# Moving the rows of the normalised x, both halves, to 64 bytes under a multiple of 1024 bytes

## The chip, the core and the metric

The kernel runs on one core of a Trainium2 chip. The metric is the time of one execution on the device in microseconds (us), lower is better; the figure of a kernel is the median of its runs.

## The reference

Two transformer blocks of two layers each, run one after the other on x (512 tokens of width 1024, fp32). The second block also carries a context of 256 tokens. Each sublayer normalises its input, scales and shifts it by vectors made from c, and multiplies the result by wide weight matrices. Cut to what the change touches:

```
h = rms_norm(x, g_norm1[l]) * (1.0 + sc1) + sh1          # block 1, attention part
u = h @ w_in[l] + b_in[l]
...
h = rms_norm(x, g_norm2[l]) * (1.0 + sc2) + sh2          # block 1, feed-forward part
up = causal_depthwise_conv(h @ w_up[l], w_conv[l], b_conv[l])
...
hx = rmsnorm(x, norm_g[i, 0]) * (1.0 + sc_x) + sh_x      # block 2, on x and on the context
hc = rmsnorm(ctx, norm_g[i, 0]) * (1.0 + sc_c) + sh_c
yx = conv_module(hx, *cp)                                # layer 0; attention in layer 1
...
fx = rmsnorm(x, norm_g[i, 2]) * (1.0 + scf_x) + shf_x
x = x + gf_x * rmsnorm(swiglu(fx, ffn_w1[i], ffn_w3[i], ffn_w2[i]), norm_g[i, 3])
```

## The kernel before, in words

Activations lie with their channels on the 128 partitions: x is `X`, eight rows (KD = 8 blocks of 128 channels) of 512 tokens in each partition. A row here is one such block in one partition, 512 fp32 numbers, 2048 bytes. The normalised x is kept as two fp32r tiles, a rounded half `Hh` and the rest `Hl` (lines 185 and 187), so that a product of fp32 accuracy is made of three fp32r matmuls:

```
def three(o, wh, wl, xh, xl, start, stop):                                      # line 433
    pe.matmul(o, wh, xh, start=start, stop=False, skip_group_check=True)        # line 435
    pe.matmul(o, wh, xl, start=False, stop=False, skip_group_check=True)        # line 436
    return pe.matmul(o, wl, xh, start=False, stop=stop, skip_group_check=True)  # line 437
```

Here a weight block of 128 columns (`wh` or `wl`, 512 bytes of a partition) is loaded into TensorE and a row of `Hh` or `Hl` moves through it; the output is one PSUM bank. A slab of weights (128 output channels, eight such blocks) comes by a DMA that SP issues into one of three `raw` tiles; ACT rounds it into `Wh` (line 2045), GpSimd (line 2534) or VectorE (line 1274) makes the rest, `Wl`. `linear` (line 449) runs the 8 x 3 matmuls of one slab on x. `linear_pair` (line 497) does two slabs at once behind a normalisation.

In the second block the context has its own halves, `hc_h` and `hc_l`, 256 tokens, rows of 1024 bytes (line 221). `linear_both` (line 466) takes, for each weight block, three matmuls on x (512 columns) and then three on the context (256 columns); `linear_pair_both` (line 477, called four times) takes x first and then the context. The feed-forward product of the second block's layer 0 has x and context side by side in one row of 768 numbers, `gb_h` and `gb_l` (line 272), and takes 512 and 256 columns of it in turn. The last attention turns its weights p into `pt2_hi` and `pt2_lo` (lines 287 and 288; pt_hi and pt_lo in the profile), rows of 256 numbers, which lie over `Hh` when that is free; the products with v are lines 1135 and 1136. GpSimd scales p (line 2579).

The places of the tiles are set by hand in one block of lines. `alloc_sbuf_tensor` puts one tile behind the other; `at` and `alloc_sbuf_tensor_at` put tiles of other stages at fixed places over them.

```
ROW = SEQ * 2                                              # line 182: 1024
assert nc.sbuf_base % ROW == 0, nc.sbuf_base               # line 183
X = sb("X", [KD, SEQ])                                     # line 184
Hh = sb("Hh", [KD, SEQ], F32R)
hl_base = nc.sbuf_base
Hl = sb("Hl", [KD, SEQ], F32R)
...
LINE = 64 / KB                                             # line 220
HC = {c0: [at(f"hc_{x}{c0}", kb - LINE, [KD, CTX], F32R) for x, kb in (("h", c0), ("l", c0 + 8))] for c0 in (0, 56)}
```

In the built program X begins at byte 27648 of each partition, Hh at 44032, Hl at 60416 and raw0 at 76800, all multiples of 1024. Wh and Wl, gb, pt_hi and pt_lo begin on multiples of 1024 too. The four hc tiles begin 64 bytes under one. The tiles `hl_base` places besides: four of the eight first weight tiles w0 (line 223), two of the five p buffers (line 281), pt_hi and pt_lo, and the tiles XT and YT of the output (lines 291 and 292).

Of the kernel before, what the change touches and what calls it, by code (L numbers as in the profile page):

```python
# [31 lines left out]
class Tally:  # L32
# [17 lines left out]
    def mark(self, name, *event, by=1):  # L50
        self.raised[name] = self.raised.get(name, 0) + by
        assert (name, event) not in self.at, (name, event)
        self.at[name, event] = self.raised[name]
        return self.sems[name], by

    def ready(self, name, *event):
        if self.known is None:
            return self.sems[name], self.at.get((name, event), 1)
        return self.sems[name], self.known[name, event]
# [34 lines left out]
def write(nc, a, out, tally):  # L94

    mark, ready = tally.mark, tally.ready
    _, SEQ, D = a["x"].shape
    CTX = a["ctx_2"].shape[1]
    DEPTH = a["w_in"].shape[0]
    KD = D // P  # L100
# [13 lines left out]
    C_QL, C_KV, C_KR, C_Q, C_K, C_V, C_GM, C_GS, _ = CUTS  # L114
# [6 lines left out]
    def sb(name, shape, dt=F32):  # L121
        return nc.alloc_sbuf_tensor(name, [P, *shape], dt)
# [3 lines left out]
    cvec = {1: sb("cvec1", [1, KD]), 2: sb("cvec2", [2, KD])}  # L126
    cact = {1: sb("cact1", [KD, 1]), 2: sb("cact2", [KD, 2])}
    MOD = {(b, l): sb(f"mod{b}_{l}", [6 * KD, b]) for b in (1, 2) for l in range(DEPTH)}
    DER = {(b, l): sb(f"der{b}_{l}", [4 * KD, b]) for b in (1, 2) for l in range(DEPTH)}


    vec_at, vec_rows = {}, []
# [36 lines left out]
    def vec(name, i=0, n=1):  # L169
        c = vec_at[name] + i  # L170
        return vcols[:, c:c + n]
# [8 lines left out]
    tap_cols = sb("tap_cols", [4, QUADS, KD])  # L180

    ROW = SEQ * 2
    assert nc.sbuf_base % ROW == 0, nc.sbuf_base
    X = sb("X", [KD, SEQ])
    Hh = sb("Hh", [KD, SEQ], F32R)
    hl_base = nc.sbuf_base
    Hl = sb("Hl", [KD, SEQ], F32R)
    RAW, WS, TM = 3, 3, 3
    raw = [sb(f"raw{i}", [8 * P]) for i in range(RAW)]
    Wh = [sb(f"Wh{i}", [8 * P], F32R) for i in range(WS)]  # L190
# [18 lines left out]
    def at(name, kb, shape, dt=F32):  # L209
        size = int(np.prod(shape)) * 4  # L210
        assert kb * KB + size <= 80 * KB, name
        return nc.alloc_sbuf_tensor_at(name, [P, *shape], dt, offset=int(base + kb * KB))
# [4 lines left out]
    XC = at("XC", 72, [KD, CTX])  # L217
    XS = {"x": X, "c": XC}
    STATS = {"x": (SV, SY, ST, SR), "c": tuple(at(f"ctx_stat{i}", 51 + i, [CTX]) for i in range(4))}
# [109 lines left out]
    def full(job):  # L329
        return ready("bank_full%d" % bank_of[job], *job)  # L330

    def free(job):
        return tally.sems["bank_free%d" % bank_of[job]], use_of[job]
# [4 lines left out]
    def empty(job):  # L338
        return tally.sems["bank_free%d" % bank_of[job]], 1

    def bank(job, n=SEQ):
        if n > SEQ:
            return banks2(job, n)
        return PS[:, bank_of[job], 0:n]

    def banks2(job, n):
        b = bank_of[job]
        return PS[:, b:b + 2, :].rearrange("p b n -> p (b n)")[:, 0:n]
# [49 lines left out]
    def _(pe):  # L398
# [287 lines left out]
        def to_tokens(job, src):  # L686

            begin(job)
            for t in range(QT):
                mm = pe.transpose(bank(job)[:, t * P:(t + 1) * P], src[:, t * P:(t + 1) * P], const("ident"))  # L690
            mm.then_inc(*fill(job))

        def last_turns(j):
# [5 lines left out]
            else:  # L699
                i = len(tally.squares) % 2  # L700
                tally.squares.append(ev)
                tally.square_free[ev] = lambda: ready("sums", ev) if j < KD - 1 else full(job)
            to_tokens(("xt", j), X[:, j, :])
            if j > 0:
# [541 lines left out]
    def _(dve):  # L1246
# [14 lines left out]
        def own(inst):  # L1261
            chain_n[0] += 1
            return after(inst, "dve_chain", chain_n[0])
# [12 lines left out]
        def mod_work(slab_n):  # L1276

            while mod_events and mod_events[0][2] <= slab_n:
                what, block_of, _, r = mod_events.pop(0)
                if what == "sum":  # L1280
                    mod_sum(block_of, r)
                else:
                    (mod_row_out if what == "row" else mod_columns)(block_of)
# [123 lines left out]
        def mod_out(b, l):  # L1407

            while any(e[1][0:2] == (b, l) for e in mod_events):
                mod_work(mod_events[0][2])  # L1410
            M, R = MOD[b, l], DER[b, l]
            dve.wait_ge(*free(("mod_t", b, l, MOD_BLOCKS - 1)))
# [9 lines left out]
        def gain(o, m, g, plus):  # L1422
            if plus:
                return own(dve.scalar_tensor_tensor(o, m, 1.0, g, ALU.add, ALU.mult))
            return own(dve.tensor_tensor(o, m, g, ALU.mult))
# [30 lines left out]
        def col(b, l, s, what, c):  # L1456
            v = 1 if s == "c" else 0
            if what < 6:
                return MOD[b, l][:, what * KD + c, v:v + 1]
            return DER[b, l][:, (what - 6) * KD + c, v:v + 1]  # L1460

# [283 lines left out]
        def mask(name):  # L1745
            return const(name).bitcast(F32)
# [33 lines left out]
        def first_gains():  # L1780
# [3 lines left out]
            dve.wait_ge(*free(("mod_t", 1, 0, 0)))  # L1784
            dve.wait_ge(*gain(DER[1, 0][:, 0:KD, 0], MOD[1, 0][:, KD:2 * KD, 0], vec(("g1", 0), 0, KD), True))

        for l in range(DEPTH):
# [83 lines left out]
            for n in range(len(tiles) + 4):  # L1871
                if n < len(tiles):
# [5 lines left out]
                    dve.wait_ge(*own(dve.tensor_tensor(d, d, mask("mask_qk"), ALU.add)))  # L1878
                    t = own(dve.tensor_reduce(mx[n % 3], bank(("s", l, h, i), (i + 1) * P), AX.X, ALU.max))
                    dve.wait_ge(*t)  # L1880
# [43 lines left out]
            def add_to_x(job, g, j):  # L1924
                dve.wait_ge(*full(job))
                dve.scalar_tensor_tensor(X[:, j, :], bank(job), g, X[:, j, :], ALU.mult, ALU.add).then_inc(*empty(job))

# [56 lines left out]
        for n in range(len(tiles) + 10):  # L1984
            if n < len(tiles):
                job = ("s2", *tiles[n])
                dve.wait_ge(*full(job))
                if n >= 3:
                    dve.wait_ge(*free(("s2", *tiles[n - 3])))
                dve.tensor_reduce(nm[n % 3], banks2(job, SEQ + CTX), AX.X, ALU.min).then_inc(*mark("neg_max2", *tiles[n]))  # L1990
            if 11 <= n < len(tiles) + 8 and n % QT == 3:
# [34 lines left out]
    def _(act):  # L2026
# [40 lines left out]
        def square(event, src, n, rows=slice(0, P), bias=0.0):  # L2067
            if event[1] == KD - 2 and ("ss", event[0]) in sums_over:
                ln_and_exp()
            if event[0] in SUMMED and event[1] == 0:  # L2070
                job = ("ss", event[0])
                if sums_over[job][1]:
                    act.wait_ge(*sums_over[job][1])
                act.activation(STATS[stream(job)][0][:, 0:n], src, ACT.Square, bias=bias).then_inc(*mark("squares", event))
                return
            i = sq_n[0]
            assert tally.squares[i] == event, (tally.squares[i], event)
            if i >= 2:
                act.wait_ge(*tally.square_free[tally.squares[i - 2]]())
            act.activation(SQ[i % 2][rows, 0:n], src, ACT.Square, bias=bias).then_inc(*mark("squares", event))  # L2080
            sq_n[0] += 1
# [117 lines left out]
        def ffn_2(l, s):  # L2199
            n, tag, name = NS[s], ("f", l, s), ("dn", 2, l, s)  # L2200
            norm_to_h(tag, n, lambda c: col(2, l, s, 3, c))
            for half in range(2):
# [11 lines left out]
                for j in range(KD):  # L2214
# [5 lines left out]
                    else:  # L2220
# [3 lines left out]
                        if j >= 2:  # L2224
                            act.wait_ge(*full(("yt", j - 2)))
                        act.activation(sl[j % 2][:, :], Y[:, j, :], ACT.Identity, scale=DER[2, l][:, 3 * KD + j, 0:1])\
                           .then_inc(*mark("y_gained", j))
# [77 lines left out]
        for l in range(DEPTH):  # L2305
# [132 lines left out]
            for j in range(KD):  # L2438
# [3 lines left out]
                act.wait_ge(*free(("wo", l, j)))  # L2442
                square((("n2", l), j), X[:, j, :], SEQ)

# [253 lines left out]
```

## Time and profile before

| what | value |
|---|---|
| median of 3 runs | 3287.12 us (3286.65 to 3288.83) |
| span of the profiled execution | 3282.0 us; its own total is not listed apart |
| TensorE busy | 3152.4 us, 96% |
| VectorE, ScalarE, GpSimd busy | 1570.4, 1186.3, 815.1 us |
| matmuls on Hh or Hl | 3 x 2208, of 512 columns |
| matmuls on hc_h or hc_l | 3 x 576, of 256 columns |

The span runs from the first to the last instruction; the time of a run also has what lies around it. The busy time of matmuls is a union: they overlap, and the duration of one (about 390 ns for 512 columns) is longer than the distance between the starts of two. The distance is read in the timeline, whose columns are the start in us from the span's begin, the duration in us, the engine, the line, the operation, output <- inputs (the moving operand first, then the weights) and the shape.

### The profile page before, as it was taken

Reading aid. Unit: us, or ns where it says so; the run is one execution under the profiler, and the core shown is the slowest. Engines: PE = TensorE matmul, PEld = TensorE weight load, DVE = VectorE, ACT = ScalarE, POOL = GpSimd, SP = SyncE. Lnnn points to the kernel's source line nnn. Section 1 sums busy time; section 2 is a strip of 40 time slices with the busy share of each in tenths; the row PEclk is TensorE's granted clock in tenths of the full one; section 3 lists DMA queues with packets and bytes.
Section 4 is the critical chain, followed back from the end, with each engine's and each line's share of the span. In section 5 each row is a group of like instructions: output and inputs, shape, how many; then the busy total and the mean of one; then the engine's idle time right before and its main releaser. Section 6 shows DMA issues by size and latency. Waiting matters only on the chain.

```text
span 3282.0 us, 38620 instructions
## 1 busy us (share of the span) xinstructions
PE 3152.4 (96%) x15546; PEld 2472.2 (75%) x15546; DVE 1570.4 (48%) x2204; ACT 1186.3 (36%) x1764; POOL 815.1 (25%) x399
## 2 busy tenths in 40 slices
PE   6999999999999999999989899999999979999998
PEld 4657778887665777778867477888888658878887
DVE  3572146464375124334378644322334899653234
ACT  3443244243444224424321244111112558632223
POOL 4302445555320343444401000000000039500000
PEclk9999999999999999999999999999999999999999
DMA  6413436665430555453335211222221110122332
GB/s 237 129 42 110 147 91 200 217 192 164 128 113 7 180 175 171 144 178 93 98 81 130 53 49 55 65 65 65 61 62 58 39 39 1 39 70 88 106 89 79
DMA packets 429892, 337.21 MB, mean 103 GB/s; under 512 B 16637, under 2 KB 411223, under 8 KB 417428
## 3 DMA queue, kind: packets, MB, share of 16 engines
q1 hardware_dynamic: 428272, 334.23, 33.5%
q8 instruction: 124, 2.03, 0.3%
q0 software_dynamic: 1248, 0.46, 0.1%
q14 instruction: 52, 0.43, 0.0%
q10 hardware_dynamic: 196, 0.07, 0.0%
HBM read 319.58 MB, written 2.10 MB: 98 GB/s over the span
## 4 chain that ended last, share of the span: by engine, by line
PE 58%; DVE 5%; POOL 4%; ACT 1%; issue 1%; SPq 0%; DMA 0%; POOLq 0%; DVEq 0%; ACTq 0%
PE PS L435 17%; PE PS L436 17%; PE PS L437 17%; POOL p L2579 4%; PE PS L524 1%; PE PS L831 1%; PE PS L592 1%; PE PS L637 1%; DVE both_tmp L1371 0%; DVE q_parts L1693 0%; PE PS L1026 0%; DVE Wl L1274 0%; PE PS L536 0%; DVE stat_t L1347 0%; SPq L2621 0%
## 5 line engine op out<-in xcount | busy, mean ns | idle before, releaser
L435 PE MATMUL PS<-Hh,Wh 128*128 128x512 f32 x2208 | 875.4, 396 | 20.5 <-DVE both_tmp L1371 8.3
L2534 POOL TENSOR_TENSOR Wl<-raw,Wh 128x1024 fp32r<-128x1024 f32 (+2 forms) x254 | 618.0, 2441 | 986.6 <-ACT Wh L2045 986.6
L436 PE MATMUL PS<-Hl,Wh 128*128 128x512 f32 x2208 | 861.8, 390 | 0.0
L437 PE MATMUL PS<-Hh,Wl 128*128 128x512 f32 x2208 | 861.4, 390 | 0.0
L2045 ACT ACTIVATE Wh<-raw 128x1024 fp32r<-128x1024 f32 (+2 forms) x442 | 436.1, 988 | 400.4 <-PE PS L437 349.5
L435 PEld LDWEIGHTS PS<-Hh,Wh 128*128 128x128 f32 x2208 | 416.1, 188 | 127.9 <-issue 62.6
L437 PEld LDWEIGHTS PS<-Hh,Wl 128*128 128x128 f32 x2208 | 415.8, 188 | 88.0
L436 PEld LDWEIGHTS PS<-Hl,Wh 128*128 128x128 f32 x2208 | 416.4, 189 | 67.6 <-issue 3.4
L1274 DVE TENSOR_TENSOR Wl<-raw,Wh 128x1024 fp32r<-128x1024 f32 (+3 forms) x188 | 217.6, 1157 | 389.6 <-ACT Wh L2045 389.3
L1952 DVE SCALAR_TENSOR_TENSOR cv<-PS,vcols,cv 128x510 f32<-128x510 f32 (+1 forms) x176 | 123.7, 744 | 216.8 <-ACT cv L2456 216.8
L435 PE MATMUL PS<-g_h,Wh 128*128 128x512 f32 x528 | 206.7, 391 | 3.5 <-POOL Wl L2534 3.5
L2564 POOL CAST k_hi<-k_ctx 64x512 fp32r<-64x512 f32 x4 | 3.6, 911 | 813.2 <-DVE k_ctx L1371 813.1
L437 PE MATMUL PS<-g_h,Wl 128*128 128x512 f32 x528 | 205.6, 389 | 0.0
L436 PE MATMUL PS<-g_l,Wh 128*128 128x512 f32 x528 | 205.5, 389 | 0.0
L435 PE MATMUL PS<-hc_h,Wh 128*128 128x256 f32 x576 | 162.7, 282 | 0.9 <-DVE hc_l L1429 0.8
L436 PE MATMUL PS<-hc_l,Wh 128*128 128x256 f32 x576 | 161.8, 281 | 0.0
L437 PE MATMUL PS<-hc_h,Wl 128*128 128x256 f32 x576 | 161.8, 281 | 0.0
L2579 POOL TENSOR_SCALAR p<-p,small 128x768 f32<-128x768 f32 x64 | 141.8, 2234 | 49.6 <-DVE small L2002 49.6
L524 PE MATMUL PS<-sq,cst 128*128 128x512 f32 (+2 forms) x244 | 119.9, 611 | 33.2 <-DVE stat_v L1344 17.6
L2456 ACT ACTIVATE cv<-PS,vcols 128x512 f32<-128x512 f32 x88 | 68.5, 779 | 192.5 <-PE PS L437 189.2
L435 PEld LDWEIGHTS PS<-hc_h,Wh 128*128 128x128 f32 x576 | 108.1, 188 | 22.5 <-DVE hc_l L1429 1.9
L436 PEld LDWEIGHTS PS<-hc_l,Wh 128*128 128x128 f32 x576 | 108.2, 188 | 20.2
(383 smaller groups left out, 4759.3 us busy)
## 6 DMA issues: line engine op xcount, KB each, us to landing
raw<-in_ffn_w SPq DMA_DIRECT2D x108, 512.0 KB, 3.6
mod_w<-in_w_mod SPq DMA_DIRECT2D x48, 1024.0 KB, 5.0
raw<-in_w_up SPq DMA_DIRECT2D x88, 512.0 KB, 4.6
mod_w<-in_w_ada SPq DMA_DIRECT2D x40, 1024.0 KB, 4.9
raw<-in_w_in SPq DMA_DIRECT2D x62, 512.0 KB, 4.0
UQ<-U SPq DMA_DIRECT2D x128, 99.4 KB, 2.2
raw<-in_w_down SPq DMA_DIRECT2D x32, 384.0 KB, 5.0
raw<-in_conv_w_pw SPq DMA_DIRECT2D x24, 512.0 KB, 4.1
```

The lines of the kernel that those rows point to most:

```text
L435: pe.matmul(o, wh, xh, start=start, stop=False, skip_group_check=True)
L436: pe.matmul(o, wh, xl, start=False, stop=False, skip_group_check=True)
L437: return pe.matmul(o, wl, xh, start=False, stop=stop, skip_group_check=True)
L524: mm = pe.matmul(bank(job, n), const(matrix)[lo:hi, :], SQ[i][lo:hi, 0:n], start=first, stop=final, skip_group_check=True)
L592: pe.matmul(PS[:, b, :], const("ident"), cst[:, 0:512], start=True, stop=True)
L637: mm = pe.matmul(PS[32 * j:32 * j + b, bank_of[job], :], cact[b][:, r, :], w[:, 512 * j:512 * (j + 1)], start=r == 0, stop=r == KD - 1, sk ...
L1274: dve.tensor_tensor(low, src, high.bitcast(F32), ALU.subtract).then_inc(*mark("w_low", k))
L1952: ins = dve.scalar_tensor_tensor(o, bank(ups[s])[:, 0:SEQ - lag], vec(("w_conv", l), tap * 2 * FC + s * FC + f), o, ALU.mult, ALU.add)
L2045: act.activation(high, src, ACT.Copy).then_inc(*mark("w_high", k))
L2456: act.activation(cv[f % 2][s][:, :], bank(job), ACT.Identity, bias=vec(("b_conv", l), s * FC + f), scale=vec(("w_conv", l), 2 * 2 * FC + s ...
L2534: pool.tensor_tensor(low, src, high.bitcast(F32), ALU.subtract).then_inc(*mark("w_low_pool", one[0]))
L2579: pool.tensor_scalar(p2[n % 5][:, :], p2[n % 5][:, :], ri2[n % 5], None, ALU.mult)\
```

## The change

Hh and Hl begin 64 bytes (16 fp32 numbers) under a multiple of 1024. The room for it comes from `der1_0` and `der1_1`, which had twice the columns they use. X, which follows the small tiles directly, begins 128 bytes lower than before; a filler of 64 bytes stands between X and Hh, another of 64 bytes behind Hl, and from raw0 on every tile is where it was.

```
--- before.py
+++ after.py
@@ -126,7 +126,7 @@
     cvec = {1: sb("cvec1", [1, KD]), 2: sb("cvec2", [2, KD])}
     cact = {1: sb("cact1", [KD, 1]), 2: sb("cact2", [KD, 2])}
     MOD = {(b, l): sb(f"mod{b}_{l}", [6 * KD, b]) for b in (1, 2) for l in range(DEPTH)}
-    DER = {(b, l): sb(f"der{b}_{l}", [4 * KD, b]) for b in (1, 2) for l in range(DEPTH)}
+    DER = {(b, l): sb(f"der{b}_{l}", [2 * b * KD, b]) for b in (1, 2) for l in range(DEPTH)}
 
 
     vec_at, vec_rows = {}, []
@@ -180,11 +180,14 @@
     tap_cols = sb("tap_cols", [4, QUADS, KD])
 
     ROW = SEQ * 2
-    assert nc.sbuf_base % ROW == 0, nc.sbuf_base
     X = sb("X", [KD, SEQ])
+    BELOW = 16
+    sb("rows_begin_below", [-nc.sbuf_base % ROW // 4 - BELOW])
     Hh = sb("Hh", [KD, SEQ], F32R)
     hl_base = nc.sbuf_base
     Hl = sb("Hl", [KD, SEQ], F32R)
+    sb("weights_begin_at", [BELOW])
+    assert nc.sbuf_base % ROW == 0, nc.sbuf_base
     RAW, WS, TM = 3, 3, 3
     raw = [sb(f"raw{i}", [8 * P]) for i in range(RAW)]
     Wh = [sb(f"Wh{i}", [8 * P], F32R) for i in range(WS)]
```

In the built program X begins at byte 27520, Hh at 43968, Hl at 60352, raw0 at 76800. Of the tiles ahead of X, der1_1, der2_0, der2_1, vcols, small and tap_cols begin 64 to 128 bytes lower. Tiles placed by `hl_base` move by 64 bytes with Hl. The instructions, their order on each engine and their waits are the same.

## Rows read from the trace of the kernel before

**Rows 1.** Page, parts 1 and 2: engines busy, granted clock in 40 slices.
```profile
PE 3152.4 (96%) x15546; PEld 2472.2 (75%) x15546; DVE 1570.4 (48%) x2204; ACT 1186.3 (36%) x1764; POOL 815.1 (25%) x399
...
PEclk9999999999999999999999999999999999999999
```

**Rows 2.** Page, part 5: the three groups of matmuls on Hh and Hl.
```profile
L435 PE MATMUL PS<-Hh,Wh 128*128 128x512 f32 x2208 | 875.4, 396 | 20.5 <-DVE both_tmp L1371 8.3
...
L436 PE MATMUL PS<-Hl,Wh 128*128 128x512 f32 x2208 | 861.8, 390 | 0.0
L437 PE MATMUL PS<-Hh,Wl 128*128 128x512 f32 x2208 | 861.4, 390 | 0.0
```

**Rows 3.** Timeline of TensorE, 2910 to 2940 us (start, us, ...); 134 rows.
```profile
2909.77 0.39 PE L436 MATMUL PS<-Hl,Wh 128*128 128x512 f32 x1
...
2939.91 0.39 PE L437 MATMUL PS<-Hh,Wl 128*128 128x512 f32 x1
```

**Rows 4.** Windows: span and us, busy us of PE, PEld, DVE, ACT, POOL, PEclk, DMA.
```profile
2910.00:2940.00 30.00, 30.00 (x134) 24.85 (x133) 13.94 (x15) 11.39 (x14) 0.00 (x0) 1.00 0.36 105
```

**Rows 5.** Timeline of all engines from 2920 us: matmuls and weight loads.
```profile
2920.19 0.39 PE L437 MATMUL PS<-Hh,Wl 128*128 128x512 f32 x1
2920.20 0.19 PEld L435 LDWEIGHTS PS<-Hh,Wh 128*128 128x128 f32 x1
...
2920.42 0.39 PE L435 MATMUL PS<-Hh,Wh 128*128 128x512 f32 x1
2920.42 0.19 PEld L436 LDWEIGHTS PS<-Hl,Wh 128*128 128x128 f32 x1
```

**Rows 6.** Timeline of TensorE, 1672 to 1676.3 us; 39 rows.
```profile
1671.76 0.28 PE L437 MATMUL PS<-hc_h,Wl 128*128 128x256 f32 x1
...
1676.23 0.28 PE L436 MATMUL PS<-hc_l,Wh 128*128 128x256 f32 x1
```

**Rows 7.** Timeline of TensorE, 2762.6 to 2765.3 us; eight rows between these.
```profile
2763.80 0.28 PE L1136 MATMUL PS<-pt_lo,v_parts 128*128 128x256 f32 x1
...
2764.88 0.60 PE L1115 MATMUL PS<-cst,p 128*128 128x128 f32 x4
```

**Rows 8.** Page, part 5: making the weight halves; matmuls on g_h.
```profile
L2534 POOL TENSOR_TENSOR Wl<-raw,Wh 128x1024 fp32r<-128x1024 f32 (+2 forms) x254 | 618.0, 2441 | 986.6 <-ACT Wh L2045 986.6
...
L2045 ACT ACTIVATE Wh<-raw 128x1024 fp32r<-128x1024 f32 (+2 forms) x442 | 436.1, 988 | 400.4 <-PE PS L437 349.5
...
L435 PE MATMUL PS<-g_h,Wh 128*128 128x512 f32 x528 | 206.7, 391 | 3.5 <-POOL Wl L2534 3.5
```

**Rows 9.** Chain that ended last, in order of time: its longest piece.
```profile
2692.89 135.27 POOL p L2579 x61
```

**Rows 10.** Instructions of line 2579: duration min/median/max in ns.
```profile
L2579 POOL TENSOR_SCALAR p<-p,small x64: 2194/2202/2573, 2690.3 to 2830.3; 128x768 f32<-128x768 f32 x64
```

**Rows 11.** Groups of VectorE, shapes apart: making Hl.
```profile
L1387 DVE SCALAR_TENSOR_TENSOR Hl<-tmp,mod,Hh 128x512 fp32r<-128x512 f32 x48 | 35.9, 747 | 2.8 <-ACT Hh L2115 1.9
...
L1387 DVE SCALAR_TENSOR_TENSOR Hl<-both_tmp,mod,Hh 128x512 fp32r<-128x512 f32 x16 | 12.0, 747 | 8.5 <-ACT Hh L2115 8.2
```

**Rows 12.** Timeline of TensorE, 2016 to 2030 us: gb, six matmuls a step.
```profile
2018.16 0.28 PE L435 MATMUL PS<-gb_h,Wh 128*128 128x256 f32 x1
...
2018.51 0.40 PE L435 MATMUL PS<-gb_h,Wh 128*128 128x512 f32 x1
...
2029.00 0.40 PE L435 MATMUL PS<-gb_h,Wh 128*128 128x512 f32 x1
```

**Rows 13.** Timeline of TensorE, 1676.6 to 1690 us: Hh, Hl and hc alternating.
```profile
1676.47 0.39 PE L435 MATMUL PS<-Hh,Wh 128*128 128x512 f32 x1
...
1677.15 0.28 PE L435 MATMUL PS<-hc_h,Wh 128*128 128x256 f32 x1
...
1677.50 0.39 PE L435 MATMUL PS<-Hh,Wh 128*128 128x512 f32 x1
...
1689.90 0.39 PE L435 MATMUL PS<-Hh,Wh 128*128 128x512 f32 x1
```

More of the change, by code:

```diff
@@ L128, in write @@
     MOD = {(b, l): sb(f"mod{b}_{l}", [6 * KD, b]) for b in (1, 2) for l in range(DEPTH)}
-    DER = {(b, l): sb(f"der{b}_{l}", [4 * KD, b]) for b in (1, 2) for l in range(DEPTH)}
+    DER = {(b, l): sb(f"der{b}_{l}", [2 * b * KD, b]) for b in (1, 2) for l in range(DEPTH)}
     vec_at, vec_rows = {}, []
@@ L182, in write @@
     ROW = SEQ * 2
-    assert nc.sbuf_base % ROW == 0, nc.sbuf_base
     X = sb("X", [KD, SEQ])
+    BELOW = 16
+    sb("rows_begin_below", [-nc.sbuf_base % ROW // 4 - BELOW])
     Hh = sb("Hh", [KD, SEQ], F32R)
@@ L187, in write @@
     Hl = sb("Hl", [KD, SEQ], F32R)
+    sb("weights_begin_at", [BELOW])
+    assert nc.sbuf_base % ROW == 0, nc.sbuf_base
     RAW, WS, TM = 3, 3, 3
```

## The prediction

> **What bounds the kernel now.** Read the page's first part and its slices first [rows 1]: TensorE is busy for 3152.4 of 3282.0 us, and its clock is granted at 9 tenths or more in all 40 slices, the upper of its two levels, 2.4 GHz. No other engine is busy for half the span. So the question is not who waits, but what one matmul costs. The costliest groups say which ones [rows 2]: the three lines of `three` with Hh or Hl as the moving operand, 2208 each, 6624 matmuls of 512 columns in all. Their mean of 390 to 396 ns is latency, not pace; matmuls overlap. The pace is the distance between two starts, and for that one reads the timeline. In an undisturbed stretch [rows 3] 134 such matmuls start between 2909.77 and 2939.91 us: 30.14 us / 133 = **226.6 ns each**. TensorE is busy for 30.00 of the 30 us from 2910 on [rows 4]: it waits for nothing there.
>
> Beside each of them the next 128 columns of weights are loaded: the load for the following matmul starts within 0.01 us of the running one [rows 5]. So there are always two streams out of SBUF, the moving row and a weight block, both of which begin on multiples of 512 bytes in the kernel before.
>
> **What a row's place is worth, by the rows there are.** No 512-column fp32r matmul of this kernel starts 64 bytes under a multiple of 1024, so the new price has to come from neighbours.
> - 256 columns from rows 64 bytes under (hc): 39 starts from 1671.76 to 1676.23 us [rows 6], 4.47 / 38 = 117.6 ns.
> - 256 columns from rows on a multiple of 1024 (pt_hi, pt_lo): nine steps from 2763.80 to 2764.88 us [rows 7], 120.0 ns.
>
> Between 226.6 ns for 512 and 120.0 ns for 256 aligned columns lie 106.6 ns for 256 columns, 2.4 columns per ns, which is the granted clock. What is left is a fixed 13.4 ns per aligned matmul at either width. The rows 64 bytes under have 117.6 - 106.6 = 11.0 ns. The difference, 2.4 ns per matmul, is the only price of this edit that the trace offers.
>
> **The change part by part.**
> 1. *Hh and Hl move by 64 bytes.* The moving rows of 6624 matmuls change their place. I take the 2.4 ns of the 256-column rows for the 512-column ones, since the fixed part was the same 13.4 ns at both widths: 6624 x 2.4 ns = **15.9 us less**. All of it lies on the path: in the stretch of [rows 3, 4] TensorE has no gap to lose it in, and what feeds it has room. A slab of weights carries 24 matmuls, 24 x 226.6 ns = 5.44 us before and 5.38 us after; its two halves take ACT 0.99 us and GpSimd 2.44 us [rows 8]. The only group of this kind that shows idle time for a weight half is another product's (g_h), 3.5 us in all [rows 8]; the matmuls on Hh waited 20.5 us, for Hh and Hl themselves [rows 2]. The bounds: nothing gained, if the 2.4 ns belong to something else than the rows' place; at most about one and a half times as much (24 us), if the wider rows gain more. On the other side the loss is bounded by the dearest rows of 512 columns, below.
> 2. *pt_hi and pt_lo lie over Hh and move too*: 384 matmuls of 256 columns, at 2.4 ns 0.9 us. I count nothing. They stand in the last attention, where the chain goes through GpSimd's scaling of p for 135.27 us [rows 9]; TensorE could be quicker there for nothing. Two of that operation's five p buffers move as well (26 of 64 calls). Its calls last 2194 to 2573 ns round a median of 2202 [rows 10]. If every moved call were as slow as the slowest, 26 x 0.37 us = 9.6 us would be lost; VectorE shows no such effect, so I take 0.
> 3. *X moves by 128 bytes, der, vcols, small and tap_cols by up to 128, two of the initial weight tiles and the output rows by 64.* For VectorE the trace has both kinds: making Hl out of tmp, whose tiles begin on multiples of 1024, takes 747 ns, and out of both_tmp, two of whose three tiles begin 64 and 128 bytes past one, 747 ns too [rows 11]. So 0 for every elementwise operation on X, Hh and Hl; most of them run beside matmuls anyway.
> 4. *der1 loses unused columns, two fillers come in.* No instruction comes, goes or changes its queue or its wait; every engine issues what it issued, in the same order.
>
> The sum: 3282.0 - 15.9 = 3266.1 us of span. The median of the three runs, 3287.12 us, lies 5.1 us above the span of the profiled execution, whose own total is not listed. With the same 5.1 us on top the forecast is **3271 us**.
>
> **The rival of no effect.** The 2.4 ns may not be the place's. The aligned 256-column rows come from bursts of twelve, with the same weights twice in a row, and there is a second aligned sample that says otherwise: the 256-column halves of gb are aligned, and three of them take 2018.16 to 2018.51 us, 0.35 us [rows 12]. Three of hc, 64 bytes under, take 1677.15 to 1677.50, also 0.35 [rows 13]. If the fixed part of a 512-column matmul has nothing to do with where its row begins, the time stays at **3287 us**. Against it: the pace in gb is uneven and an aligned burst settles at 120.0 ns.
>
> For this rival speaks a rule. The Trainium skill, "TensorE: Matmul & The Clock Gate", Part 2 (step 1, LDWEIGHTS), says that TensorE reads the moving operand and the weights through two independent SBUF ports, so that a weight load takes nothing from a running matmul. By that rule two streams never meet, no offset between them matters, and the sum would be 3287. The same page gives a warm back-to-back gap of columns / 2.4 + 2.5 ns, about 216 ns for 512; the trace has 226.6 ns, so something beyond its formula is paid for here on every matmul.
>
> **The rival that ends slower.** The rows of hc may be cheap not because they lie 64 bytes under a boundary, but because they lie off the rows of Hh between which they are taken. `linear_both` alternates three matmuls of 512 columns on x with three of 256 on the context. Thirteen such sixes take 1676.47 to 1689.90 us [rows 13], 1033 ns each. In gb, where both kinds begin on multiples of 1024, ten sixes take 2018.51 to 2029.00 us [rows 12], 1049 ns each. Since three narrow ones take 0.35 us in both, those 16 ns sit on the 512-column ones. After the change Hh and hc have the same place again. If equality is what hurts, each of the 512 interleaved sixes (576 groups of three on hc, less 4 x 16 that `linear_pair_both` runs by themselves) pays 16 ns: 8.2 us more, **3295 us**, while plain stretches keep 226.6 ns. It decides if the pace in a six goes above 1042 ns. A harsher form is that 512-column rows off the boundary lose those 16 ns per three everywhere: 2208 x 16 ns = 35 us, **3322 us**. For both: the dear 512-column rows exist, and no trace shows a 512-column row off the boundary that is cheap. Against both: in a stretch of hc alone, where all rows have the same place, the pace is 117.6 ns and not dearer.
>
> That the change doesn't do what it says can be left out: the built program has Hh at byte 43968 and Hl at 60352 of each partition, 64 under 43 and 59 times 1024, and the weights where they were.
>
> **How the numbers follow.** A measurement of this kernel can tell some 0.2% from no change, 6.6 us: faster is under 3280.5 us, slower over 3293.7. The forecast of a cheaper fixed part has 0.45, since the two cleanest stretches of equal width differ in just this; its own range is 3263 (one and a half times the price) to 3279 (half of it), with some 0.05 for a larger gain. No effect has 0.25, for the equal 0.35 us in the two mixed stretches. The sixes that pay again have 0.18, the loss in all 512-column rows 0.12. So faster 0.45, same 0.25, slower 0.30. The range goes from 3259 to 3300: it takes in the first three cases with a few us on either side for parts 2 and 3, and leaves out the loss everywhere and a gain well above the price, 0.17 together.
>
> **What would show it.** In the timeline of a stretch like [rows 3], the distance of starts on Hh and Hl: 224.2 ns if the forecast holds, 226.6 if there is no effect, 230 or more in the harsh case. In sixes of Hh and hc: 1026 ns by the forecast, 1033 without effect, 1049 by the slower rival. In gb nothing moves, so its 1049 ns has to stay; that is the check that a difference comes from the rows' place. The scaling of p should keep its median of 2202 ns. The forecast is wrong if the pace of 512 columns stays or rises, or if it falls and the span does not follow, which would mean that TensorE was not what bound those stretches.

## The result and the profile after

The changed kernel takes 3319.34 us (median of four runs, 3317.29 to 3320.74) against 3287.97 us of the kernel before on the same chip: a ratio of 1.0095, 95% interval 1.0081 to 1.0109. It is slower by 31.4 us, by the interval 26.6 to 35.8 us. The forecast was 3271 us, the range ended at 3300: wrong in sign. The harsher form of the second rival had 3322 us.

The profiled execution has a span of 3315.5 us and took 3317.29 us itself. Three lines were added ahead of the helpers, so line 435 is now 438, and so on. The page's parts 1, 2 and 4, beside [rows 1], and behind them part 4 of the kernel before (shares of the span in the chain of work that ended last):

```profile
PE 3191.5 (96%) x15546; PEld 2477.4 (75%) x15546; DVE 1571.8 (47%) x2204; ACT 1188.0 (36%) x1764; POOL 807.6 (24%) x399
...
PEclk9999999999999999999999999999999989999999
...
PE 61%; DVE 6%; ACT 2%; issue 1%; SPq 0%; POOL 0%; DMA 0%; DVEq 0%; ACTq 0%
```

```profile
PE 58%; DVE 5%; POOL 4%; ACT 1%; issue 1%; SPq 0%; DMA 0%; POOLq 0%; DVEq 0%; ACTq 0%
```

TensorE is busy 39.1 us longer; GpSimd is busy 7.5 us less, the rest within 5.2 us of before. The chain went through GpSimd's scaling of p for 4% of the span before; now GpSimd has 0% of it, and TensorE 61% for 58%. One slice of the clock has an 8, and the mean granted clock is 0.985, where it was 0.987. The profile of the first experiment below has such a slice too and 0.984, and it is not slower, so the clock is not the cause. The time is in the matmuls. Their groups, beside [rows 2] and the one on g_h in [rows 8] (g_h did not move):

```profile
L438 PE MATMUL PS<-Hh,Wh 128*128 128x512 f32 x2208 | 885.9, 401 | 18.0 <-DVE both_tmp L1374 8.3
L440 PE MATMUL PS<-Hh,Wl 128*128 128x512 f32 x2208 | 875.1, 396 | 0.0
L439 PE MATMUL PS<-Hl,Wh 128*128 128x512 f32 x2208 | 875.0, 396 | 0.0
...
L438 PE MATMUL PS<-g_h,Wh 128*128 128x512 f32 x528 | 206.7, 392 | 3.4 <-POOL Wl L2537 3.4
```

The three groups on Hh and Hl are longer by 5 to 6 ns a matmul, the one on g_h by 1 ns. No wait has grown: the idle time ahead of L438 is 18.0 us, where it was 20.5. The pace, in the timeline of the same stage as [rows 3] (134 rows again), and the windows of that stretch, to be read beside [rows 4]:

```profile
2942.99 0.39 PE L438 MATMUL PS<-Hh,Wh 128*128 128x512 f32 x1
...
2974.03 0.39 PE L439 MATMUL PS<-Hl,Wh 128*128 128x512 f32 x1
```

```profile
2943.00:2973.00 30.00, 30.00 (x130) 24.07 (x129) 11.60 (x13) 9.39 (x12) 0.00 (x0) 1.00 0.36 106
```

31.04 us / 133 = **233.4 ns**, where it was 226.6. TensorE is again busy for all of the 30 us at full clock, and 130 matmuls fit where 134 did. The other stretches of the prediction, in the timeline of the kernel after:

```profile
1695.32 0.28 PE L440 MATMUL PS<-hc_h,Wl 128*128 128x256 f32 x1
...
1700.08 0.28 PE L440 MATMUL PS<-hc_h,Wl 128*128 128x256 f32 x1
...
1701.24 0.39 PE L438 MATMUL PS<-Hh,Wh 128*128 128x512 f32 x1
...
1714.80 0.39 PE L438 MATMUL PS<-Hh,Wh 128*128 128x512 f32 x1
...
2042.15 0.40 PE L438 MATMUL PS<-gb_h,Wh 128*128 128x512 f32 x1
...
2053.70 0.40 PE L438 MATMUL PS<-gb_h,Wh 128*128 128x512 f32 x1
...
2795.92 0.28 PE L1138 MATMUL PS<-pt_hi,v_parts 128*128 128x256 f32 x1
...
2797.17 0.28 PE L1139 MATMUL PS<-pt_lo,v_parts 128*128 128x256 f32 x1
```

| stretch | before | after |
|---|---|---|
| Hh, Hl alone, ns a matmul | 226.6 [rows 3] | 233.4 |
| hc alone (not moved) | 117.6 [rows 6] | 4.76 us / 42 = 113.3 |
| pt_hi, pt_lo | 120.0 [rows 7] | 1.25 us / 11 = 113.6 |
| six on Hh, Hl and hc, ns | 1033 [rows 13] | 13.56 us / 13 = 1043 |
| six on gb (not moved) | 1049 [rows 12] | 11.55 us / 11 = 1050 |

So 512 columns lost 6.7 ns, 256 columns gained 4 to 6 (hc without having been moved), and gb, the control, kept its pace. A three is one call of `three`, a six is a three on x and the three on the context behind it. By all rows of the two traces, 1619 threes of Hh and Hl are followed by another such three: from start to start they went from 680 to 700 ns at the median, and from 1120.0 to 1152.7 us in sum, 32.8 us more. 496 sixes went from 1033 to 1045 ns at the median, and from 514.6 to 519.1 us in sum, 4.5 us more. 60 threes on hc alone, 13 ns shorter each at the median, gave back 0.6 us in sum. Together that is 36.7 us; the spans differ by 33.5, the medians by 31.4.

### The profile page after: what moved, and what is told of

The parts are those of the page before. It is cut to its first block, busy times and chain, and to the rows that moved or that the text cites. A ratio compares the mean times of both kernels' runs of the same rounds, so it can differ in the third digit from the quotient of the medians.

```text
span 3315.5 us, 38620 instructions
## 1 busy us (share of the span) xinstructions
PE 3191.5 (96%) x15546; PEld 2477.4 (75%) x15546; DVE 1571.8 (47%) x2204; ACT 1188.0 (36%) x1764; POOL 807.6 (24%) x399
## 4 chain that ended last, share of the span: by engine, by line
PE 61%; DVE 6%; ACT 2%; issue 1%; SPq 0%; POOL 0%; DMA 0%; DVEq 0%; ACTq 0%
PE PS L438 17%; PE PS L439 17%; PE PS L440 17%; PE PS L527 1%; PE PS L834 1%; PE PS L595 1%; PE PS L1138 1%; PE PS L1107 1%; PE PS L640 1%; PE PS L1118 1%; PE PS L1139 1%; DVE both_tmp L1374 0%; PE PS L1108 0%; DVE q_parts L1696 0%; ACT sq L2083 0%
## 5 line engine op out<-in xcount | busy, mean ns | idle before, releaser
L438 PE MATMUL PS<-Hh,Wh 128*128 128x512 f32 x2208 | 885.9, 401 | 18.0 <-DVE both_tmp L1374 8.3
L440 PE MATMUL PS<-Hh,Wl 128*128 128x512 f32 x2208 | 875.1, 396 | 0.0
L439 PE MATMUL PS<-Hl,Wh 128*128 128x512 f32 x2208 | 875.0, 396 | 0.0
L438 PEld LDWEIGHTS PS<-Hh,Wh 128*128 128x128 f32 x2208 | 416.7, 189 | 135.4 <-issue 60.0
L438 PE MATMUL PS<-g_h,Wh 128*128 128x512 f32 x528 | 206.7, 392 | 3.4 <-POOL Wl L2537 3.4
L438 PE MATMUL PS<-hc_h,Wh 128*128 128x256 f32 x576 | 162.4, 282 | 0.6 <-DVE hc_l L1432 0.5
L438 PEld LDWEIGHTS PS<-hc_h,Wh 128*128 128x128 f32 x576 | 108.2, 188 | 25.1 <-DVE hc_l L1432 1.7
```

## The experiments

### Everything but the rows' place

Hh and Hl go back to multiples of 1024; X, the small tiles and der stay as changed.

```
-    sb("rows_begin_below", [-nc.sbuf_base % ROW // 4 - BELOW])
+    sb("rows_begin_below", [-nc.sbuf_base % ROW // 4])
...
-    sb("weights_begin_at", [BELOW])
```

> The change with Hh and Hl left on multiples of 1024: only X, der, vcols, small and tap_cols move. Theory A (the place of the 512-column rows): pace on Hh and Hl back at 226.7 ns, time 3287 to 3289 us. Rival R (X or the small tiles, which the vector engines read, cost the time): pace of TensorE's starts stays as before, but the time is near 3319 us.

Measured: 3286.66 us against 3287.30, ratio 0.9999 (0.9989 to 1.0009). The timeline, 133 rows from the first to the last of these:

```profile
2913.94 0.39 PE L438 MATMUL PS<-Hl,Wh 128*128 128x512 f32 x1
...
2943.86 0.39 PE L438 MATMUL PS<-Hl,Wh 128*128 128x512 f32 x1
```

29.92 / 132 = 226.7 ns. The loss belongs to the place of Hh and Hl and of what is placed with them; X, the small tiles and der (parts 3 and 4 of the change) cost nothing. The initial weight tiles and the output rows went back with Hl here, and no run moves them alone. The span of this profile is 3289.5 us, 7.5 above that of the kernel before, with equal medians: its granted clock is 0.984 against 0.987, and the 17 runs of the kernel before beside it go from 3283 us at 0.987 to 3293 at 0.984. So single spans are good to some 8 us here.

### Only Hl below

Hl lies first, 64 bytes under; Hh begins on a multiple of 1024.

```
-    Hh = sb("Hh", [KD, SEQ], F32R)
-    hl_base = nc.sbuf_base
     Hl = sb("Hl", [KD, SEQ], F32R)
-    sb("weights_begin_at", [BELOW])
+    sb("hh_begins_at", [BELOW])
+    Hh = sb("Hh", [KD, SEQ], F32R)
+    hl_base = nc.sbuf_base - 4 * KD * SEQ
```

> The change with Hl alone 64 bytes under; Hh on a multiple of 1024 (Hl now lies first, Hh behind it; the two lie at the two ends of the same room). Theory A1 (each row's own place sets what its matmul costs): only the third matmul in three that streams Hl is dear, about 10.5 us over before, 3298 us; two distances of 226.7 ns and one of 233.3 ns in three. Theory A2 (what counts is whether neighbouring rows have the same place): another pace than either kernel, for all three distances; if unequal places are good as with hc between Hh, 3287 us or less, if they are bad, above 3298 us.

Measured: 3297.87 us, ratio 1.0040 (1.0027 to 1.0053). The timeline, again 133 rows:

```profile
2917.05 0.39 PE L438 MATMUL PS<-Hh,Wh 128*128 128x512 f32 x1
...
2947.26 0.39 PE L438 MATMUL PS<-Hh,Wh 128*128 128x512 f32 x1
```

30.21 / 132 = 228.9 ns: a three takes 686.6 ns, which is 2 x 226.7 + 233.3. Time and sum are those of a price on the moved row alone, but the three distances are not 226.7, 226.7 and 233.3; each is about 229, so the price isn't paid at the row that has it. The sixes alternate between 1043 and 1057 ns, mean 1051: worse than with both halves moved (1045). That the time is the expected 3298 us is partly chance: in the trace the threes add 11 us and the sixes, which the expectation left out, 7.6 us more, while the medians differ by 10.6. What gave back the rest was not followed up; the granted clock of this profile is 0.988, against 0.984 in the first experiment.

### The weights moved too

raw, Wh and Wl also begin 64 bytes under a multiple of 1024, so that row and weight block stand to each other as before.

```
     Hl = sb("Hl", [KD, SEQ], F32R)
-    sb("weights_begin_at", [BELOW])
-    assert nc.sbuf_base % ROW == 0, nc.sbuf_base
     RAW, WS, TM = 3, 3, 3
...
+    sb("stats_begin_at", [BELOW])
+    assert nc.sbuf_base % ROW == 0, nc.sbuf_base
```

> The change with the weights moved by the same 64 bytes (raw, Wh and Wl), so that rows and weight blocks have the same relation as in the kernel before. Theory B (the relation of row and weight block counts): the pace on Hh and Hl is 226.7 ns again, while products on rows left on multiples of 1024 (g, mg, yml, ysb, q_parts, ql: 2616 matmuls of 512 columns) now go at 233.3 ns, 17 us; time about 3305 us. Theory A (the row's own place counts): 233.3 ns on Hh and Hl, 226.7 ns on g, time about 3319 us.

Measured: 3297.87 us, ratio 1.0037 (1.0023 to 1.0050). The timeline (133 rows), and the timelines of two other products whose rows stayed on multiples of 1024, g (31 rows) and q_parts (25 rows):

```profile
2918.87 0.39 PE L438 MATMUL PS<-Hh,Wh 128*128 128x512 f32 x1
...
2948.79 0.39 PE L438 MATMUL PS<-Hh,Wh 128*128 128x512 f32 x1
```

```profile
3050.27 0.39 PE L438 MATMUL PS<-g_h,Wh 128*128 128x512 f32 x1
...
3057.14 0.39 PE L438 MATMUL PS<-g_h,Wh 128*128 128x512 f32 x1
```

```profile
2851.19 0.40 PE L438 MATMUL PS<-q_parts,Wh 128*128 128x512 f32 x1
...
2856.79 0.40 PE L438 MATMUL PS<-q_parts,Wh 128*128 128x512 f32 x1
```

29.92 / 132 = 226.7 ns, with the rows 64 bytes under, as the theory of the relation has it. **It is not where a row begins that costs, but where it begins against the weight block.** The time expected from it, 3305 us, was too high. It put 6.7 ns on every row that stayed, but these lie 64 bytes past the weights now and not under them: g runs at 6.87 us / 30 = 229.0 ns, q_parts at 5.60 us / 24 = 233.3, both at 226.7 before. That two products with the same distance have two paces is not explained. From start to start, g, q_parts and the smaller products on such rows (mg, yml, ysb, ql) add 6 us, and the 496 sixes, which the sum had left out, add 7.5: in them rows, context and weights all begin alike now. A place for the weights is thus a place for all products at once.

### A probe of places

1470 matmuls ahead of the first slab of the first product, 70 series of 21 (seven threes): a width, an offset into Hh and Hl and one into the weights for each series. They write into a free PSUM bank that nothing reads.

```
+    for n, hi, lo, at_w in PROBES:
+        for r in range(7):
+            wh, wl = (x[:, r * P + at_w // 4:(r + 1) * P + at_w // 4] for x in wf)
+            xh, xl = (x[:, r * SEQ + o // 4:r * SEQ + o // 4 + n] for x, o in zip(flat, (hi, lo)))
+            three(PS[:, b, 0:n], wh, wl, xh, xl, r == 0, r == 6)
```

> The kernel before with 70 series of 21 extra matmuls (seven blocks of three, as in the products) put in ahead of one slab; their results are not used. Each series has its own width, place of the moving rows and place of the weight block. Theory A: 512 columns at 226.7 ns on a multiple of 1024 and 233.3 ns at 960 bytes past one, with any weight place; 256 columns 120 ns and about 114 ns. Theory B: with the weight block 448 bytes past its place (64 under the next), the rows at 960 go at 226.7 ns and those at 0 at another pace. If the end of the row counts rather than its begin, 496 columns from 0 (which end 64 bytes under) and 496 columns from 960 change places.

Measured, in the timeline: of each series the 7th and the 19th start, so the difference / 12 is the settled distance. In this order: 512 columns with rows at 768 and weights at 0; rows 960, weights 0; rows 0, weights 64; rows 960, weights 448; then 256 columns with rows at 768 and at 960, weights at 0.

```profile
133.42 0.39 PE L436 MATMUL PS<-Hh,Wh 128*128 128x512 f32 x1
...
136.14 0.39 PE L436 MATMUL PS<-Hh,Wh 128*128 128x512 f32 x1
...
143.10 0.40 PE L436 MATMUL PS<-Hh,Wh 128*128 128x512 f32 x1
...
145.90 0.40 PE L436 MATMUL PS<-Hh,Wh 128*128 128x512 f32 x1
...
197.41 0.39 PE L436 MATMUL PS<-Hh,Wh 128*128 128x512 f32 x1
...
200.21 0.39 PE L436 MATMUL PS<-Hh,Wh 128*128 128x512 f32 x1
...
231.37 0.39 PE L436 MATMUL PS<-Hh,Wh 128*128 128x512 f32 x1
...
234.09 0.39 PE L436 MATMUL PS<-Hh,Wh 128*128 128x512 f32 x1
...
184.39 0.28 PE L436 MATMUL PS<-Hh,Wh 128*128 128x256 f32 x1
...
185.83 0.28 PE L436 MATMUL PS<-Hh,Wh 128*128 128x256 f32 x1
...
189.36 0.28 PE L436 MATMUL PS<-Hh,Wh 128*128 128x256 f32 x1
...
190.72 0.28 PE L436 MATMUL PS<-Hh,Wh 128*128 128x256 f32 x1
```

They give 226.7, 233.3, 233.3, 226.7, 120.0 and 113.3 ns. The same reading for the other series, by the distance of row and weight block in bytes, modulo 256 (row place / weight place in brackets):

| row less weights, mod 256 | 512 columns, ns | 256 columns, ns |
|---|---|---|
| 0 | 226.7 (256/0, 512/0, 768/0, 960/448), 227.1 (0/256) | 120.0 (768/0, 0/256, 960/448) |
| 64 | 228.9 (64/0, 0/448), 228.8 (960/128) | 117.8 (64/0, 960/128), 113.3 (0/448) |
| 128 | 233.3 (128/0, 384/0, 896/0), 232.6 (0/128, 960/64) | 118.8 (128/0, 960/64), 118.3 (0/128) |
| 192, which is 64 under | 233.3 (192/0, 960/0, 0/64, 960/256) | 117.8 (192/0, 0/64), 113.3 (960/0, 960/256) |

For 512 columns each row of the table has one price in this probe, to 0.7 ns, however the distance comes about. The very first series, 512 columns at 0/0, is left out: it came down to 226.7 ns only behind its 10th start. For 256 columns the order is reversed: rows in line with the weights are the dearest of the table. Between these widths, rows at 0 and at 960 with weights at 0: 384 columns 173.3 and 173.3 ns, 480 columns 216.7 and 215.8, 496 columns 223.3 and 226.7, 504 columns 227.1 and 226.7. So there is no loss at 480 columns, half of it at 496, none at 504 and all of it at 512: it does not simply grow with the width. Nor is it the row's end that counts: 496 columns from 0 end 64 bytes under a multiple of 1024 and are the cheaper of the two. Two series moved one half alone: with Hl at 960 a matmul takes 228.8 ns, as in the run with only Hl moved, and with Hh at 960 it takes 234.4, more than with both moved. The price of a three is thus not the sum of the prices of its rows.

### A probe of sixes and of narrower weight blocks

The same probe, with series of seven sixes (512 columns at place a, 256 at place b), and of threes whose weight blocks have 96, 64 or 32 columns.

```
+    for step in PROBES:
+        for r in range(7):
+            for n, x, at_x, which, at_w, m in step:
+                pe.matmul(PS[0:m, b, 0:n], wf[which][:, r * P + at_w // 4:r * P + at_w // 4 + m],
+                          flat[x][:, r * SEQ + at_x // 4:r * SEQ + at_x // 4 + n], start=r == 0, stop=r == 6,
+                          skip_group_check=True)
```

> The kernel before with 51 more series of extra matmuls ahead of one slab (results not used): sixes of 512 and 256 columns at chosen places, weight blocks of 96, 64 and 32 columns, weight halves at unequal places, and places 4 to 96 bytes off. Theory B (row and the weight block that is loaded beside it meet in SBUF, by their relation): with fewer weight columns the part of the distance beyond columns / 2.4 shrinks in proportion, at 512 columns from 13 ns to about 4 ns with 32, and more at the dear place (20 ns) than at the cheap one; rows and weights moved together by 64, 128 or 192 bytes go at 226.7 ns; rows at 0 with only the third block moved make two distances dear or none. Theory A (the row's own place): weight width and weight place change nothing. For the sixes: 1033 ns at (0, 960) and 1049 ns at (0, 0) as in the products; with (960, 960), the change's own pair, about 1043 ns or more.

Measured, in the timeline: sixes with 512 columns at 0 and 256 at 960 (five from the first row to the second), both at 960 (five), and threes of 512 columns with rows and weights both moved by 64 (7th and 19th start).

```profile
131.60 0.39 PE L463 MATMUL PS<-Hh,Wh 128*128 128x512 f32 x1
...
136.77 0.39 PE L463 MATMUL PS<-Hh,Wh 128*128 128x512 f32 x1
...
167.19 0.39 PE L463 MATMUL PS<-Hh,Wh 128*128 128x512 f32 x1
...
172.41 0.39 PE L463 MATMUL PS<-Hh,Wh 128*128 128x512 f32 x1
...
304.09 0.39 PE L463 MATMUL PS<-Hh,Wh 128*128 128x512 f32 x1
...
306.81 0.39 PE L463 MATMUL PS<-Hh,Wh 128*128 128x512 f32 x1
```

1034 ns, 1044 ns and 226.7 ns. The first two are the kernel before and the kernel after in small. In the last three sixes of their series, both at 0 give 1050.7 (gb's case), 960 and 0 give 1054.3. With the 512 columns at 0, the narrow rows at 16, 32 or 128 give 1053.3, at 64 1045.0, and at 192, as at 960, 1033.3. So it is not equality that makes a six dear: most unequal places cost as much as equal ones, and equal at 960 is cheaper than 960 and 0. Of all pairs tried none is under 1033. So the places of the kernel before were the best ones for a six among those tried. Rows and weights moved together by 32, 64, 96, 128, 160 or 192 are at 226.7 to 227.2 ns from the 10th to the 19th start. By the same starts the narrower weight blocks did not shrink the excess in proportion (rows at 0: 230.2, 229.4 and 231.6 ns for 96, 64 and 32 columns; at 960: 228.1, 232.6, 231.3): that a load takes turns from the row in proportion to its size is not borne out. With 96 columns of weights the rows at 960 are even the cheaper ones.

### The context on a multiple of 1024

The kernel before, with the hc tiles 64 bytes higher, so that Hh, Hl, hc and the weights all begin alike.

```
-    LINE = 64 / KB
+    LINE = 0
```

> The kernel before with the context's rows back on multiples of 1024: hc and Hh have the same place, both in the good relation to the weights. If equality of neighbouring rows hurts in a six, as the gb rows suggested, each of 512 sixes costs 16 ns more: 8 us, 3295 us, and the loss sits on the 512-column matmuls. If only the relation of each row to the weights counts, the 512-column ones keep 226.7 ns and the 256-column ones go from 117.7 to 120 ns: 1728 x 2.3 ns = 4 us, 3291 us.

Measured: 3292.96 us against 3290.68, ratio 1.0010 (1.0001 to 1.0018). The timeline, six sixes of Hh, Hl and hc from the first row to the second:

```profile
1685.22 0.40 PE L435 MATMUL PS<-Hh,Wh 128*128 128x512 f32 x1
...
1691.53 0.40 PE L435 MATMUL PS<-Hh,Wh 128*128 128x512 f32 x1
```

6.31 / 6 = 1052 ns, and Hh and Hl by themselves stay at 680 ns a three. So the loss in sixes that the second rival forecast is real, some 18 ns a six, and it sits where the rival put it: in a six of this trace without a wait the first two matmuls of 512 columns stand 234.7 and 234.4 ns before the next start, where they had 227.0 in the kernel before, and the three narrow ones take 353 ns as before. In sum the 496 sixes go from 514.6 to 522.3 us, 7.7 more; the interval of the time allows 0.3 to 5.9. From the first matmul on gb to the last the run is 5.0 us longer (518.3 to 523.3 us), but from the first on hc to the first on gb 2.0 us shorter than in the first experiment (343.5 to 341.5). That stretch ran at another granted clock, as its windows show for the first experiment and for this run (columns as in [rows 4]):

```profile
1678.30:2021.80 343.50, 325.62 (x1962) 241.45 (x1961) 243.04 (x329) 104.65 (x159) 14.30 (x6) 0.97 0.30 78
```

```profile
1679.50:2020.90 341.40, 323.30 (x1961) 239.72 (x1960) 243.33 (x329) 104.81 (x159) 13.65 (x6) 0.99 0.30 79
```

So part of what the sixes lose comes back at the clock, 0.99 for 0.97. Why the clock differs is open.

### Only pt below

pt_hi and pt_lo 64 bytes under, the two p buffers over them 1024 bytes higher; Hh and Hl in place.

```
...
-    pt2_hi = [nc.alloc_sbuf_tensor_at(f"pt2_hi{i}", [P, KT, 2 * P], F32R, offset=int(hl_base - (16 - 6 * i) * KB)) for i in range(2)]
+    pt2_hi = [nc.alloc_sbuf_tensor_at(f"pt2_hi{i}", [P, KT, 2 * P], F32R, offset=int(hl_base - (16 - 6 * i) * KB + KB - 64)) for i in range(2)]
...
```

> The kernel before with pt_hi and pt_lo alone 64 bytes under a multiple of 1024 (the p buffers behind them move by 1024). In the changed kernel their distance fell from 120.0 to about 114.2 ns. If that stretch is bound by TensorE, 384 x 5.8 ns = 2.2 us less, 3285 us; if GpSimd's scaling of p sets its pace, no difference, 3287 us.

Measured: 3291.14 us against 3290.68, ratio 0.9997 (0.9988 to 1.0006). The timeline, seven rows:

```profile
2763.89 0.28 PE L1136 MATMUL PS<-pt_lo,v_parts 128*128 128x256 f32 x1
...
2764.57 0.28 PE L1136 MATMUL PS<-pt_lo,v_parts 128*128 128x256 f32 x1
```

0.68 / 6 = 113.3 ns, 120.0 in [rows 7]. Inside the bursts of the 384 matmuls the median distance goes from 120 to 114 ns, and the kernel is not quicker, as part 2 had it: GpSimd has 4% of the chain in this run too. That it has 0% in the changed kernel is not the place of pt: it is 0% in the run with the context moved as well, where pt lies as before. In both the granted clock of that stage is 0.97, where it is 0.99 here and in the kernel before.

### Wide and narrow threes apart

If pure threes cost 680 and 340 ns, a six need not cost 1033. In the kernel before, `linear_both` and the product on gb run all threes on x first, then those on the context.

```
-            for i in range(KD):
-                mm = both(job, w, i, slice(0, P), (Hh[:, i, :], Hl[:, i, :]), (hc[0][:, i, :], hc[1][:, i, :]),
-                          i == 0, i == KD - 1)
+            for s in "xc":
+                for i in range(KD):
+                    mm = both(job, w, i, slice(0, P), (Hh[:, i, :], Hl[:, i, :]), (hc[0][:, i, :], hc[1][:, i, :]),
+                              i == 0, i == KD - 1, s)
...
```

> The kernel before, every tile in its old place, but in linear_both and in the product on gb all threes of 512 columns of a slab run first and the threes of 256 columns after them (in the kernel before they alternate). Nothing is left out. By the probes a mixed six costs 1033 ns (hc 64 bytes under) or 1050 (gb in line with the weights), while pure threes of 512 cost 680. If the pure threes on hc run at 113.3 ns a matmul, as in the changed kernel, a six's worth costs 680 + 340 = 1020 ns: 512 x 13 = 6.7 us less on hc, and on gb 680 + 360 = 1040 against 1050, 176 x 10 = 1.8 us less; 8.5 us together. If hc keeps the 117.7 ns that its pure stretches have in the kernel before, 680 + 353 = 1033 is what the six costs already: only gb gains, 1.8 us, which can't be told from no change. The rows of 512 columns have to stay at 226.7 ns and the scaling of p at 2202 ns. The output of the x part comes before the context part, but the pair of banks is still released as one, so no wait should change.

Measured: 3288.80 us against 3285.66, ratio 1.0010 (1.0000 to 1.0019). The timeline: 48 matmuls on hc, and the first matmuls of two slabs that follow each other (eight threes of each kind between them):

```profile
1679.13 0.28 PE L435 MATMUL PS<-hc_h,Wh 128*128 128x256 f32 x1
...
1684.66 0.28 PE L437 MATMUL PS<-hc_h,Wl 128*128 128x256 f32 x1
...
1684.78 0.39 PE L435 MATMUL PS<-Hh,Wh 128*128 128x512 f32 x1
...
1693.05 0.39 PE L435 MATMUL PS<-Hh,Wh 128*128 128x512 f32 x1
```

5.53 / 47 = 117.7 ns: hc stayed at the dearer of its two paces, so a slab takes 8.27 us / 8 = 1034 ns for what was a six, as before. The gain expected on gb did not come either. There TensorE now reaches the last rows on x before VectorE has made them, as in this row, and a stretch of 192 matmuls on gb takes 34.6 us where it took 33.7:

```profile
2213.55 0.50 PE L435 MATMUL PS<-gb_h,Wh 128*128 128x512 f32 x1 [0.94 <-DVE gb_l L1431]
```

No version here beats the kernel before.

## Why the prediction was wrong

**What failed is the first step of part 1**, "I take the 2.4 ns of the 256-column rows for the 512-column ones, since the fixed part was the same 13.4 ns at both widths". The reading of 117.6 against 120.0 ns was right, and the probe widens it (113.3 to 117.8 against 120.0). But the fixed part is equal at both widths only in line with the weights: 120.0 - 106.7 and 226.7 - 213.3 are both 13.3 ns, with columns / 2.4. At 64 under it is 6.7 (or 11.0) ns for 256 columns and 20.0 for 512. The equality at one place was taken as evidence for the other place, where no row of 512 columns stood. In the place of -2.4 ns x 6624 = -15.9 us stand +6.7 ns a matmul in 1619 pure threes, 32.8 us in sum with their waits, and 4.5 us in sixes.

**The bounds were better than the use made of them.** The upper one, the dear rows in gb, gave 3322 us, 2.7 us from the median. It was left outside the range with a chance of 0.12. That it comes so near is partly luck: its 16 ns were those of rows in line with the weights that alternate with narrow ones, and what was paid is 20 ns in pure threes and 9 in sixes. The one argument against it, that hc alone runs at 117.6 ns and not dearer, was about 256 columns again: the same carry-over, used twice. Its reason was off as well. Not "off the boundary" is dear: with the weights moved too, rows off the boundary run at 226.7 ns.

**The rival of equal places** has its number, but not its reason. With Hh and hc both in line with the weights a six costs 18 ns more, 16 were forecast from gb; by the probe of sixes, though, unequal places are as dear. After the change the two are equal again, 64 under, and a six costs 1043 to 1045 ns, past its point of 1042. But pure threes at the new paces, 700 and 340 ns, would be 1040 already, so most of that is the price of the wide rows. And plain threes did not keep their pace, as this rival had it; the sixes are 4.5 us of the loss and not the main thing.

**The rival of no effect** fell: the same rows, at 960, have 226.7 ns with weights at 448 and 233.3 with weights at 0. By the Trainium skill, "TensorE: Matmul & The Clock Gate", Part 2 (step 1, LDWEIGHTS), row and weights come through two independent SBUF ports, and a load takes nothing from the running matmul. That their relative place would not matter, as the prediction took from it, the trace does not bear out. Whether it is a port, a bank or something else that they share, no run here shows.

**What held.** That TensorE's pace sets the time: the span followed the distance of starts, with no new wait. Part 2: pt became quicker and the stage did not. The scaling of p stayed, beside [rows 10]:

```profile
L2582 POOL TENSOR_SCALAR p<-p,small x64: 2199/2213/2328, 2717.4 to 2855.8; 128x768 f32<-128x768 f32 x64
```

Part 3: making Hl takes 748 ns, where it took 747 [rows 11]. The 5.1 us between span and median were mostly the spread of runs: the execution profiled after took 1.8 us more than its span.

## What to carry to other kernels

A price read at one shape of an instruction holds for that shape: before it is multiplied by thousands, find or make one row of the shape that it is meant for, and where there is none let the dearest row of that shape into the range. When a buffer is moved, ask what streams beside it: here the distance between moving row and weight block, modulo 256 bytes, moved the pace, and streams of 512-column rows were quickest with it at 0. A probe of a thousand extra matmuls in a running kernel, with the place stepped from series to series, answers that in one run, if each series is long enough to settle and the widths and the mix are those of the kernel.

## What the runs showed that was not expected

- The price of a place turns round with the width. 64 under the weights, 256 columns go from 120.0 to 113.3 or 117.8 ns, 384 stay at 173.3, and 512 go from 226.7 to 233.3.
- One and the same stretch has two paces. hc, neither it nor its weights moved, runs at 117.6 ns before [rows 6] and at 113.3 after; in the probes 256 columns at 960 settle at 113.3, at 192 once at 117.8 (behind a series at 128) and once at 113.3 (behind one at 960). Each was kept to the end of its stretch. For 512 columns, too, one distance has two paces: with the weights moved g runs at 229.0 and q_parts at 233.3 ns. In the kernels where hc ran at 117.7 the matmuls ahead were 512-column ones in line with the weights, in the kernel after ones 64 under; that what runs ahead decides was not tested by itself.
- Offsets under 64 bytes count too, and not symmetrically: 512 columns at 16 take 231.7 ns, at 1008 (16 under) 226.7, at 4 238.0.
- A price is shared out among neighbours: with only Hl moved the three matmuls of a group are each some 2.3 ns later, not one of them 6.7.
- The paces that settle fully, 113.3, 120.0, 226.7 and 233.3 ns, are 17, 18, 34 and 35 times 6.67 ns. What steps in that unit stays open, as does why 512 columns miss a step where 256 gain one.
